# A first norm whose sums, root and reciprocal are taken during the compression, and an input that is turned at pairs of chunks

## What is computed

```python
def rms_norm(x, g):
    y = xf * lax.rsqrt(jnp.mean(xf * xf, axis=-1, keepdims=True) + NORM_EPS)
    return (y * g.astype(jnp.float32)).astype(x.dtype)
...
x = x + 0.5 * swiglu(rms_norm(x, norm_gain[l, 0]), ffn_in[l, 0], ffn_out[l, 0])
```

```python
for c in range(n_sub):
    hid = hid + jnp.einsum('bphf,fe->bphe', pieces[:, c:c + n_cmp], w1[c])
return jnp.einsum('bnhe,ed->bnhd', jax.nn.silu(hid), w2)
```

## Time and profile before

| | before |
|---|---|
| median of 3 runs | 1693.51 us (1692.31 to 1696.29) |
| the profiled execution | 1691.56 us, of which the profile's span is 1689.8 us |
| PE busy | 1590.7 us, 94% |
| DVE busy | 816.6 us, 48% |
| ACT busy | 656.8 us, 39% |
| TensorE clock granted, mean | 0.978 of full speed |

### The profile page before, as it was taken

The page is one execution under the profiler, slowest core; times in us unless marked ns, Lnnn a source line. Parts: engine busy times, 40 slices in busy tenths (PEclk is TensorE's granted clock), DMA queues, the critical chain, the costliest instruction groups (busy, mean ns, idle before and its releaser), DMA issues.

```text
span 1689.8 us, 28006 instructions
## 1 busy us (share of the span) xinstructions
PE 1590.7 (94%) x11347; PEld 1478.7 (88%) x11347; DVE 816.6 (48%) x1527; ACT 656.8 (39%) x1172; POOL 121.6 (7%) x155
## 2 busy tenths in 40 slices
PE   4999998999999999999987998999798999999998
PEld 3778886999999999999976776777697999999998
DVE  4777779533433335436458995222356333233331
ACT  4556665322214332233335654555414342122221
POOL 0000000000000000001052002333000000000000
PEclk9999999999999999999977999999998999999999
DMA  8324230335434354242224005999122233232331
GB/s 314 117 107 193 100 124 27 124 125 186 157 117 149 124 174 140 88 154 90 79 77 129 1 1 143 255 258 260 49 88 63 76 98 103 71 88 77 106 90 66
DMA packets 183753, 202.27 MB, mean 120 GB/s; under 512 B 9894, under 2 KB 167309, under 8 KB 181069
## 3 DMA queue, kind: packets, MB, share of 16 engines
q1 hardware_dynamic: 167637, 111.67, 21.9%
q0 software_dynamic: 11680, 89.10, 15.5%
q10 hardware_dynamic: 4352, 0.34, 0.2%
HBM read 195.86 MB, written 31.40 MB: 134 GB/s over the span
## 4 chain that ended last, share of the span: by engine, by line
PE 84%; DVE 9%; ACT 3%; issue 2%; SPq 1%; DMA 1%; POOL 0%; ACTq 0%; DVEq 0%; PEldq 0%; POOLq 0%
PE PS L852 19%; PE PS L854 19%; PE PS L853 19%; PE PS L806 3%; PE PS L808 3%; PE PS L807 3%; PE PS L790 3%; PE PS L1209 2%; PE PS L1162 1%; PE PS L1137 1%; PE PS L1185 1%; SPq L595 1%; PE PS L1190 1%; ACT DEC L1531 1%; PE PS L1227 1%
## 5 line engine op out<-in xcount | busy, mean ns | idle before, releaser
L852 PE MATMUL PS<-HNH,WHI 128*128 128x272 f32 x1408 | 408.8, 290 | 7.6 <-DVE HNL L1759 6.7
L853 PE MATMUL PS<-HNL,WHI 128*128 128x272 f32 x1408 | 406.7, 289 | 0.0
L854 PE MATMUL PS<-HNH,WLO 128*128 128x272 f32 x1408 | 406.3, 289 | 0.0
L852 PEld LDWEIGHTS PS<-HNH,WHI 128*128 128x128 f32 x1408 | 267.1, 190 | 10.3 <-issue 7.8
L1333 ACT ACTIVATE WHI<-WR 128x1024 fp32r<-128x1024 f32 (+3 forms) x144 | 164.7, 1152 | 278.4 <-DMA WR<-in_ffn_in 128.9
L1677 DVE TENSOR_TENSOR WLO<-WR,WHI 128x1024 fp32r<-128x1024 f32 (+3 forms) x144 | 192.4, 1342 | 157.3 <-ACT WHI L1333 156.6
L853 PEld LDWEIGHTS PS<-HNL,WHI 128*128 128x128 f32 x1408 | 267.8, 190 | 0.0
L854 PEld LDWEIGHTS PS<-HNH,WLO 128*128 128x128 f32 x1408 | 267.6, 190 | 0.0
L1685 DVE TENSOR_TENSOR PT<-PS,PT 64x512 fp32r<-64x512 f32 x256 | 176.4, 689 | 66.3 <-ACT PT L1340 63.3
L852 PE MATMUL PS<-HIDH,WHI 128*128 128x272 f32 x704 | 202.4, 287 | 0.0
L854 PE MATMUL PS<-HIDH,WLO 128*128 128x272 f32 x704 | 202.4, 287 | 0.0
(11 more groups left out here) (366 smaller groups left out, 2507.7 us busy)
## 6 DMA issues: line engine op xcount, KB each, us to landing
WR<-in_ffn_in SPq DMA_DIRECT2D x88, 512.0 KB, 3.7
WR<-in_ffn_out SPq DMA_DIRECT2D x32, 704.0 KB, 4.3
out_dil_s<-in_cache_dil_kv POOLq DMA_DIRECT2D x8, 2044.0 KB, 9.1
WR<-in_w_in SPq DMA_DIRECT2D x14, 648.0 KB, 4.3
BIG<-in_cache_dil_kv SPq DMA_DIRECT2D x8, 512.0 KB
WR<-in_w_out SPq DMA_DIRECT2D x8, 512.0 KB, 3.6
out_dil_s<-in_cache_dil_kv POOLq DMA_DIRECT2D x8, 508.0 KB, 5.0
out_win_s<-in_cache_win_kv POOLq DMA_DIRECT2D x8, 508.0 KB, 5.3
```

Source lines behind the costliest of these rows:

```text
L852: pe.matmul(out, a[0], b[0], start=first, stop=False)
L853: pe.matmul(out, a[0], b[1], start=False, stop=False)
L854: return pe.matmul(out, a[1], b[0], start=False, stop=last)
```

## The change

The norm's squares go from the odd steps 49 to 63 of DVE to steps 24, 28, ... 52. Its sums go on PE from chunk 63 to chunk 58 (`x_sums`), with the same 544 columns laid out as 512 and 32, in the two PSUM banks that `second` uses; so `second(14)` now waits for the root as well. The root goes on ACT from step 63 to step 59, in two instructions ahead of `silu(14)`; the reciprocal on DVE from step 63 to step 60. The nine slices of x are turned at chunks 5, 6, 9, 10, 13, 14, 17, 18, 21 in place of 5, 7, 9, ... 21.

```diff
+        RBf, SQAf = (t.rearrange("p h t -> p (h t)") for t in (RB, SQA))
...
-        X_AT = lambda i: 5 + 2 * i
+        X_AT = lambda i: 5 + 4 * (i // 2) + i % 2
...
+            def x_sums():
+
+                pe.wait_ge(ld["const"], 16)
+                pe.wait_ge(rs[0]["sq"], 1)
+                pe.wait_ge(w_copied, 2 * NB - 2)
+                pe.matmul(PS[:, 6, :], ones, SQAf[:, 0:TP], start=True, stop=True)
+                pe.matmul(PS[:, 7, TP // 2:TP // 2 + NS], ones, SQAf[:, TP:T], start=True, stop=True)\
+                    .then_inc(rs[0]["sum"], 1)
+
             def second(n):
                 kv = n % 2
                 if n == 0:
                     pe.wait_ge(ld["small"], SMALL)
+                if n == 2 * NB - 2:
+                    pe.wait_ge(rs[0]["root"], 1)
                 pe.wait_ge(silu_done, n + 1)
...
-                elif X == NCH - 1:
-                    after = {0: lambda: rms(0)}
+                if X == NCH - 6:
+                    after[0] = x_sums
...
-                    rms(0)
+                if X == NCH - 5:
+                    act.wait_ge(ld["const"], 16)
+                    act.wait_ge(rs[0]["sum"], 1)
+                    act.activation(RBf[:, 0:TP], PS[:, 6, :], ACT.Sqrt, bias=eps, scale=1.0 / D)
+                    act.activation(RBf[:, TP:T], PS[:, 7, TP // 2:TP // 2 + NS], ACT.Sqrt, bias=eps, scale=1.0 / D)\
+                        .then_inc(rs[0]["root"], 1)
                 if X % 4 == 3:
                     silu(X // 4)
...
-                if X % 2 and X >= NCH - 16:
-                    square(0, (X + 16 - NCH) // 2)
+                if X % 4 == 0 and NCH // 2 - 8 <= X < NCH - 8:
+                    square(0, (X + 8 - NCH // 2) // 4)
                 if X == NCH - 1:
 
                     remain(0, KD * P)
                     remain(1, KD * P)
+                if X == NCH - 4:
                     inverse()
```

## The result

The changed kernel takes 1713.37 us (median of 4 runs, 1712.27 to 1715.43), before 1693.54 us in the same comparison: ratio 1.0116, 95% interval 1.0099 to 1.0134. It is 19.8 us slower. The profiled execution has a span of 1712.5 us, 22.7 longer than before's.

The account below looks back on a forecast made before the run. PE was taken to bound the kernel (84% of the span). Pairs +11.6 - 3.9, squares +2.7, end +2.2 make +12.6; clock +7.5 makes +20 us, forecast 1713.5 us, range for 8 in 10 1705 to 1718.

Parts of the forecast that it names:

- Pairs: Turning of x, chunks 6, 10, 14, 18: PE waits 2.9 us each for the copy, +11.6; `second`'s four waits go, -3.9.
- The clock: Compression: PE stops six times for 2.9 to 3.2 us; half clock costs 1.5 us at five of them, +7.5.
- the slow stretches are longer: Rival, half clock behind PE's stops: lasts twice as long, up to six times 1.7 us more, 1718 to 1726; 8%.
- The rival in which the clock holds: PE's stops: all waits come, but at most two lower the clock, +12.6 to +15.6, 1706 to 1709; 20%.
- Squares: DVE steps 28 to 52: seven squares don't fit beside `rows_out` by 0.39 us each, +2.7, between 0 and 3.5.
- Sums in chunk 58: PE, chunk 58: the sums have no wait to hide them, +0.9 us, between 0.8 and 1.1.
- The root in front of `silu(14)`: ACT: two table loads and the root delay Silu to 277.5, `second(14)` waits, cover 0.45 us: +3.1.
- the reciprocal in step 60: DVE: the 3.55 us reciprocal delays chunk 63's low parts, so chunk 63 waits until 286.2: +3.2 us.
- a drain about as long as the load at each switch: Rival, ACT's table switches: `second(14)` waits 5.9 us in place of 3.1, +23 in all, 1716; 4%.
- The gain at the end: Start of chunk 63 to first feed-forward matmul: 7.35 us in place of 12.34, a gain of 5.0.
- The seven waits for low parts: Sign in PE's waits: `hidden`'s first matmul waits for DVE's low parts some seven times, about 0.4 us each.
- The rival in which the new waits are given back: Compression: DVE and ACT run ahead during PE's waits and PE catches up; all given back is -8 us, 1685.5; 5%.

Follow-up runs that it names:

- experiment 5: Kernel of before with only the slices of x turned in pairs, plus 22 unread matmuls on PE ahead of each of the four waits; 1701.69 us, ratio 1.0044.
- experiment 2: The changed kernel with the slices of x turned at chunks 5, 7, ... 21 as before; 1699.67 us, ratio 1.0039 against before.
- experiment 3: Kernel of before with only the squares moved to steps 24, 28, ... 52; 1693.31 us, ratio 1.0003.
- experiment 8: Against before: slices at 4, 6, ... 20, squares at 26, 30, ... 54, sums in chunk 62, root and reciprocal at 61, weight parts earlier; 1685.37 us, ratio 0.9957.

## Why the prediction was right, step by step

It said 1713.5, and 1713.37 was measured; the steps mostly bear that out, with errors that cancel.

- **Pairs**, 11.6 of wait less 3.9. Right in mechanism, and nearly in size: chunk 6's wait is 2.9 from its group's end to the turning, and experiment 5, where only that is left, gives +7.0 in the trace against 7.7. The waits of `second` were worth 4.8 from chunk start to chunk start and not the 3.9 of the earlier trace rows: a row of waits gives the idle time, and PE's start behind a wait costs a little more each time.
- **The clock**, five of six stops at 1.5 us. The mechanism is shown by experiment 5. All six stops of the changed kernel, 2.7 to 3.0 us each, were followed by half clock, and the four at the pairs cost 7.4 where four at 1.5 would be 6. Chunk by chunk against experiment 5 it is 1.6, 1.6, 1.5 and 2.8: behind the fourth the clock was low for 6.8 us, the rival "the slow stretches are longer", come true at one stop of six. That was no new behaviour: the kernel before had gone to half clock at 292.0, behind the stop that ended at 291.39, and stayed there until 298.8, also 6.8 us (over the next stop too). The prediction read one half-microsecond of that stretch and took its length from the other, at 923. Shorter stops of PE went without: the clock stays at 1.00 behind the 1.81 of experiment 2. The Trainium skill's rule (page "TensorE: Matmul & The Clock Gate", part 1) that activity releases the throttle is what the filled kernel shows: matmuls of no use kept the clock at 1.00. The rival in which the clock holds would have ended at 1706 to 1709, and is out.
- **Squares**, 2.7 predicted, 2.0 measured (experiments 2, 3 and the changed kernel alike). The place and the count of seven were right, the term was mis-sized, 0.28 a time and not 0.39. DVE's timeline in the changed kernel shows why:

```profile
171.88 0.42 DVE L1711 COPY VV<-PS 128x256 f32<-128x256 f32 x1
172.22 4.22 DVE L1702 TENSOR_TENSOR PT<-PS,PT 64x512 fp32r<-64x512 f32 x6
```

  The next instruction starts 0.34 us behind the copy's start. The 0.46 of the prediction came from a row of before (138.33, the next instruction at 138.78) in which the high part that this one needs was ready only at 138.71.
- **Sums in chunk 58**, 0.9 predicted, 1.1 measured.
- **The root in front of `silu(14)`** and **the reciprocal in step 60**. Timeline of the changed kernel there, ACT, PE, DVE, to hold against the earlier trace rows:

```profile
292.66 1.28 ACT L1395 ACT_TABLE_LOAD   x1
293.96 0.69 ACT L1395 ACTIVATE GB<-PS,CO 128x512 f32<-128x512 f32 x1
294.54 0.28 ACT L1396 ACTIVATE GB<-PS,CO 128x32 f32<-128x32 f32 x1
294.84 1.28 ACT L1363 ACT_TABLE_LOAD   x1
296.13 0.69 ACT L1363 ACTIVATE BIG<-PS,B 128x510 f32<-128x510 f32 x1
...
296.92 1.33 PE L839 MATMUL PS<-W,BIG 128*128 128x64 f32 x8 [2.95 <-issue]
309.96 0.50 PE L807 MATMUL PS<-PT,CW1H 128*128 128x512 f32 x1 [2.69 <-DVE PT L1702]
315.19 1.10 PE L839 MATMUL PS<-W,BIG 128*128 128x64 f32 x8 [0.78 <-ACT BIG L1363]
318.77 0.56 PE L864 MATMUL PS<-HNH,WHI 128*128 128x272 f32 x1 [2.47 <-DVE HNL L1777]
...
303.18 3.55 DVE L1688 RECIPROCAL GB<-GB 128x544 f32<-128x544 f32 x1
306.76 0.42 DVE L1711 COPY VV<-PS 128x256 f32<-128x256 f32 x1
307.11 2.80 DVE L1702 TENSOR_TENSOR PT<-PS,PT 64x512 fp32r<-64x512 f32 x4
```

  The detour runs as added up, and there is no drain between root and table load: 292.66 to 296.82 is 4.16 for the five, the sum of their durations within 0.1. The piece of 32 columns took 0.28, of which 0.11 lies inside the one before; the 0.17 left is near the 0.2 that was taken. The rule of the Trainium skill's page "ScalarE: Activation LUTs" (section "What ACT_TABLE_LOAD costs"), a drain about as long as the load at each switch, is not seen here, where by the prediction's estimate it would have cost 2.8 us, and that rival is out. PE's wait was 2.95 (3.1 predicted), chunk 63's 2.69 or 2.8 from start to start (3.2 predicted). That PE waits less because the half clock in chunks 60 and 61 (297.6 to 301.0) makes it arrive later is argued, not tried; in the two traces of experiment 2's kernel, where that stretch began 1.7 and 1.4 us behind the stop and not 0.7, the wait was 1.81 and 2.1.
- **The gain at the end**, 5.0 predicted, 3.5 measured. The path is as it was added up: 7.43 and 7.45 us in the two traces of the changed kernel without pairs, 7.42 in experiment 8, all with the clock at 1.00 from the start of chunk 63 to `second(15)`. In the changed kernel it took 8.81, with the clock at half from 311.3 to 314.7, inside chunk 63, 1.3 us behind the wait that the reciprocal made.
- **The sum.** Without the clock +12.6 was predicted. The traces give 11 to 12: 14.4 - 7.4 = 7.0 at the pairs, 2.0 for the squares, and 2.2 to 2.8 at the end, the prediction's own figure and the most that experiment 2 leaves for it. No run has the end without any half clock, so this part isn't measured by itself. The squares were 0.7 off and the pairs, through the waits of `second`, 0.7 too, both to the dear side. The clock was 7.5 in the prediction and is about 10 here: 7.4 at the pairs, and 5.1 less 2.2 to 2.8 at the end. So the hit within 0.2 us is luck: errors of 1 to 3 us of opposite sign stand behind it, and the interval of the timing, 1.0099 to 1.0134, is itself 6 us wide. The mechanism is not luck: each of the predicted places shows its loss.

Two of the signs that the prediction named did not come. The seven waits for low parts stand in no list of PE's waits, though each costs 0.25 to 0.29 us; and the path from chunk 63 took 8.8 and not 7.4.

The rival in which the new waits are given back is out: up to chunk 63 the delay of the changed kernel never shrinks by more than 1.2 us from one chunk to the next, and it does so only where a wait of `second` was removed (another 0.44 goes at the chunks from which a slice was moved away); what comes back behind chunk 63, 3.5, is the gain at the end.

## What to carry to other kernels

Work that is moved off the last step under a stage's cover goes into queues that are served in order: ask of each queue what stands directly behind it, and by what margin that was in time. Here the margins were 0.45 us on ACT, 0.13 us on DVE, and below zero at the pairs; in experiment 8, which puts these steps one or two chunks elsewhere, none of the new waits is left. Where PE is the bound, count a stop such as those here, 2.7 to 3.0 us, as the stop and another 1.5 us or so of half clock, 2.8 in one case of four. A distance from one chunk's first matmul to another's, in both traces, finds small losses that a list of waits leaves out (seven times 0.25 to 0.29 us stood in no row).

## What the hardware showed that was not expected

- Matmuls of no use made a kernel faster: 88 of them, some 11 us of PE work (4 x 2.77), 6.7 us less in all.
- The start of the compression differs from execution to execution by up to 1.7 us where the code is the same (chunk 0 in experiments 2 and 7), and this is the clock too, although the profile doesn't say so. In the changed kernel's profile chunk 0 took 5.42 us, in before's 3.73, and the view prints 1.00 for both. But the trace of the changed kernel has no record of the clock ahead of 31.35 us, and the view prints 1.00 where there is none. The matmuls tell it: up to there one of 512 columns takes 0.63 us, behind it 0.40, and 0.63 is what they take in experiment 3 where half clock is on record (28.8 to 32.2 us). The changed kernel, then experiment 3 and its clock:

```profile
28.63 0.63 PE L809 MATMUL PS<-PT,CW1L 128*128 128x512 f32 x1
31.73 0.40 PE L809 MATMUL PS<-PT,CW1L 128*128 128x512 f32 x1
...
29.34 0.63 PE L808 MATMUL PS<-PT,CW1L 128*128 128x512 f32 x1
```

```profile
29.00:29.50 0.50, 0.50 (x3) 0.50 0.72 303
```
